# Loading a weight stream in neighbouring pairs of chunks: one 1 MB transfer into two of four slots, in place of two of 512 KB

## The reference, cut to what matters

```python
for l in range(DEPTH):                            # 2 layers
    mc = adaln(c_ctx, ada_w[l], ada_b[l])         # silu(c) @ ada_w: (1024) x (1024, 6144)
    ml = adaln(c, ada_w[l], ada_b[l])             # shift, scale, gate for both halves of the layer
    h = modulate(x, norm_mix[l], m[0], m[1])      # rmsnorm(x) * (1 + scale) + shift
    y = retention_mixer(h, ...) if l == 0 else attention(h, ...)
    x = x + m[2] * y
    h = modulate(x, norm_ffn[l], m[3], m[4])
    a = conv3(h @ ffn_w_in[l]); u, g = split(a)   # D_FF = 2816
    x = x + m[5] * ((silu(g) * u) @ ffn_w_out[l])
y = rmsnorm(x, norm_final)
```

## Time and profile before

| | us |
|---|---|
| median of 3 runs | 2169.85 (2168.47 to 2174.03) |
| the profiled execution | 2169.51 |
| its span | 2167.7 |
| TensorE busy (PE, 12352 matmuls) | 2075.3 (96%) |
| VectorE busy | 957.8 (44%) |
| ScalarE busy | 654.2 (30%) |
| GpSimd busy | 662.3 (31%) |
| mean granted clock of TensorE | 0.977 |

### The profile page before, as it was taken

How to read it: one execution, slowest core, us unless ns; L and a number is a source line. 1 busy time by engine, 2 the same in 40 slices (tenths; PEclk the granted TensorE clock), 3 DMA queues, 4 the chain that set the end, 5 groups by cost and what they waited for, 6 DMA issues and landing times.

```text
span 2167.7 us, 32212 instructions
## 1 busy us (share of the span) xinstructions
PE 2075.3 (96%) x12352; PEld 1816.5 (84%) x12352; DVE 957.8 (44%) x1420; ACT 654.2 (30%) x1282; POOL 662.3 (31%) x400
## 2 busy tenths in 40 slices
PE   5899999999999998999999999899989999999998
PEld 2776887698588757999999999895559999999998
DVE  1502420340241044662564363657651773574473
ACT  2432222212222314331232233334432432232232
POOL 2333233223323313333323324430004433333332
PEclk8899999999999998999999999899999999999999
DMA  6532232222233201442432342220002122222221
GB/s 251 182 123 68 102 113 68 97 91 85 68 108 107 69 31 52 142 144 76 139 136 87 107 145 69 67 82 1 1 1 69 58 78 78 69 77 78 68 68 50
DMA packets 52440, 190.01 MB, mean 88 GB/s; under 512 B 5872, under 2 KB 7152, under 8 KB 51696
## 3 DMA queue, kind: packets, MB, share of 16 engines
q1 hardware_dynamic: 47232, 171.99, 23.7%
q10 hardware_dynamic: 5104, 16.53, 2.0%
HBM read 181.41 MB, written 7.08 MB: 87 GB/s over the span
## 4 chain that ended last, share of the span: by engine, by line
PE 90%; issue 2%; DVE 2%; DMA 1%; ACT 1%; POOL 1%; POOLq 1%; ACTq 0%; DVEq 0%; SPq 0%
PE ps L349 35%; PE ps L388 21%; PE ps L364 16%; PE ps L700 2%; PE ps L404 2%; PE ps L331 2%; PE ps L540 2%; PE ps L549 1%; PE ps L666 1%; PE ps L683 1%; PE ps L535 1%; PE ps L336 1%; PE ps L422 1%; DMA raw<-stream_dram 1%; PE ps L412 1%
## 5 line engine op out<-in xcount | busy, mean ns | idle before, releaser
L1042 POOL TENSOR_TENSOR w_l<-raw,w_h 128x1024 fp32r<-128x1024 f32 x232 | 563.6, 2431 | 1323.4 <-ACT w_h L735 1323.1
L349 PE MATMUL ps<-h_h,w_h 128*128 128x320 f32 x1696 | 527.6, 311 | 3.6 <-issue 2.1
L349 PE MATMUL ps<-h_h,w_l 128*128 128x320 f32 x1696 | 524.1, 309 | 0.0
L349 PE MATMUL ps<-h_l,w_h 128*128 128x320 f32 x1696 | 523.9, 309 | 0.0
L735 ACT CAST w_h<-raw 128x1024 fp32r<-128x1024 f32 x232 | 245.6, 1059 | 580.4 <-PE ps L388 315.2
L349 PEld LDWEIGHTS ps<-h_h,w_h 128*128 128x128 f32 x1696 | 318.4, 188 | 16.8 <-issue 15.2
L349 PEld LDWEIGHTS ps<-h_l,w_h 128*128 128x128 f32 x1696 | 318.5, 188 | 0.2 <-issue 0.2
L349 PEld LDWEIGHTS ps<-h_h,w_l 128*128 128x128 f32 x1696 | 318.4, 188 | 0.0
L1192 DVE SCALAR_TENSOR_TENSOR xT<-ps,mods,xT 128x128 f32<-128x128 f32 (+2 forms) x264 | 108.0, 437 | 302.2 <-PE ps L388 302.2
L1333 DVE SCALAR_TENSOR_TENSOR cc<-ca,vec,cc 128x641 f32<-128x641 f32 x88 | 231.3, 2629 | 15.2 <-issue 15.2
L388 PE MATMUL ps<-m_l,w_h 128*128 128x320 f32 x704 | 217.0, 308 | 0.0
(11 more groups left out here) (186 smaller groups left out, 2706.7 us busy)
## 6 DMA issues: line engine op xcount, KB each, us to landing
raw<-stream_dram SPq DMA_DIRECT2D x328, 512.0 KB, 3.5
S<-state_dram ACTq DMA_DIRECT2D x4, 1024.0 KB, 7.5
new_state_dram<-st_out ACTq DMA_DIRECT2D x8, 512.0 KB, 3.1
xT<-x_dram ACTq DMA_DIRECT2D x1, 2560.0 KB, 11.7
y_dram<-aq ACTq DMA_DIRECT2D x8, 320.0 KB, 2.4
dm<-diff_dram ACTq DMA_DIRECT2D x1, 512.0 KB, 4.0
rope_t<-rope_t_dram ACTq DMA_DIRECT2D x1, 512.0 KB, 7.6
rope_a<-rope_a_dram ACTq DMA_DIRECT2D x1, 512.0 KB, 3.5
```

The source lines that it names most:

```text
L349: mm = nc.tensor.matmul(ps[:, banks + half, 0:HALF], w, x[:, k, lo_hi(half)], start=(k == 0 and n == 0), stop=(k == KT - 1 and n == 2))
L1042: nc.gpsimd.tensor_tensor(w_l[:, r, :], raw[:, s, :], w_h[:, r, :].bitcast(F32), ALU.subtract).then_inc(raw_used[s], 1)
```

## The change

Neighbouring chunks c and c + 1 (c even) are loaded by one DMA of 1 MB into slots c % 4 and c % 4 + 1. SP waits for `raw_used` of both slots first. The two slots of a pair share one landing semaphore, so whoever waits for either chunk waits for the whole megabyte. The stream lies in memory pair by pair, with 8 KB in a row for each partition. There are 164 DMAs in place of 328. Nothing else differs: `raw_landed[s]` is now a name for the pair's semaphore, and the counts that consumers wait for are the same, since each slot is still filled once in every four chunks.

```diff
-        raw_landed = [sem(f"raw_landed{s}") for s in range(RAW)]
+        pair_landed = [sem(f"pair_landed{s}") for s in range(RAW // 2)]
+        raw_landed = [pair_landed[s // 2] for s in range(RAW)]
...
             def load(c, i, turns):
-                s = c % RAW
                 if turns is not None:
-                    sp.wait_ge(raw_used[s], turns)
-                sp.dma_start(raw[:, s, :], dr["stream"][c + RAW * i]).then_inc(raw_landed[s], 16)
-
-            for c in range(RAW):
+                    sp.wait_ge(raw_used[c], turns)
+                    sp.wait_ge(raw_used[c + 1], turns)
+                sp.dma_start(raw[:, c:c + 2, :], dr["stream"][c // 2 + RAW // 2 * i]).then_inc(pair_landed[c // 2], 16)
+
+            for c in range(0, RAW, 2):
                 load(c, 0, None)
             with sp.Fori(1, CHUNKS // RAW) as i:
-                for c in range(RAW):
+                for c in range(0, RAW, 2):
                     load(c, i, i)
...
     stream = np.concatenate(parts)
     assert stream.shape == (CHUNKS, P, CH), stream.shape
+    stream = stream.reshape(CHUNKS // 2, 2, P, CH).transpose(0, 2, 1, 3)
```

## The result

| | before | after |
|---|---|---|
| median, us | 2171.19 (4 runs) | 2195.85 (4 runs, 2195.27 to 2198.67) |
| the profiled execution | 2169.51 | 2195.84 |
| its span | 2167.7 | 2194.1 |

The ratio is 1.0112, with a 95% interval of 1.0100 to 1.0125: 24 us slower, where 23 were forecast. Every page line of the changed kernel stands one line lower in the file (L303 is the load, L405 the block).

What follows compares the result with a forecast made beforehand. TensorE was taken as the bound, with 90% of the chain; loads cost only where they land late. Blocks 21.9 plus start 1.5 gave 23.4 us on 2169.5, so 2192.9, stated as 2193; range 2183 to 2208.

Steps and rivals of the forecast that it cites:

- The forecast's 14 blocks: Blocks behind the start whose last a chunk has its cover used up or nearly so; together 21.9 us longer.
- start, to the block at 102.37: Program start, loads on the chain: chunks 10 and 11 +0.7, first four m chunks +0.8; sum +1.5, between -2 and +5.
- the v blocks of heads 0 to 3: Attention's v blocks: heads 1 to 3 lose 5.0 us together, head 0 loses 1.1.
- E: Extra landing time of a pair's second 512 KB: 1.25 us, so a pair lands 4.65 us after issue.
- `S` as an upper bound: The 1 MB load of `S` took 7.2 us, bounding the extra landing time from above at 3.8.
- The rivals at E = 0 and 3.8: A pair lands as fast as a chunk: 2174, chance 0.06; or it lands like `S`: 2233, chance 0.06.
- the fourth, a megabyte in 4 KB pieces: Rival: the megabyte goes out as 4 KB pieces at full cost, 2193 to 2199; chance 0.05.
- a2's 0.43 us: In late blocks the third a chunk, wanted 0.43 us before the fourth, lands with it and adds that much.
- the first turns of the second and third group: Two feed-forward blocks whose fourth a chunk lands 0.33 us after the start; 1.18 us each, 2.4 together.
- "Cost 0" for the casts behind a block: First m chunk behind a block: ScalarE's cast ends 1.7 us later, but ScalarE's next work moves equally; cost 0.
- The rival of a gain at the start: The start is bandwidth-bound and gains 3.7 us at the higher rate: 2188; chance 0.08.

Runs made afterwards that it cites:

- Giving the cover back: Changed kernel with its feed-forward blocks one m chunk later (ten of the eleven move): 1.0076 to the kernel before, 16 to 17 us slower.
- The shared landing alone: Kernel before, still with single 512 KB loads, but the two chunks of a pair share a semaphore and consumers wait for both: 1.0024, 5 us.
- the constants first: Changed kernel with ScalarE issuing the load of the constants ahead of that of x: 1.0101 to the kernel before, 21 to 22 us.
- joint issue with separate landings: SP waits for both slots of a pair as in the change, then issues two 512 KB loads with a semaphore each: 1.0088 to the kernel before, 19 us.

## Why the prediction was right

**Place and mechanism.** The forecast's 14 blocks are the 14 that became longer, and the six others behind the start still take 1.92 us. Behind the last block only 1.1 us are lost, to the granted clock (below). Giving the cover back brought the feed-forward blocks back to 1.92; the kernel with only the blocks in pairs puts 14 of the 24 us there (10 to 19).

**Where the 26.3 us between the two profiled executions are:**

| | forecast | profile after |
|---|---|---|
| start, to the block at 102.37 | 1.5 | 4.9 |
| the v blocks of heads 0 to 3 | 6.1 | 0.7 + 0.9 + 0.8 + 1.0 = 3.4 |
| the first stalled feed-forward block (887.20) | 1.7 | 3.3 |
| the other nine | 14.1 | 12.2 |
| between the blocks and behind them | 0 | 2.5 |
| sum | 23.4 | 26.3 |

So the sum is right in part by luck: two terms were too large, two too small, and one was missing.

**E was too small.** 1.25 was forecast from two loads of 512 KB, and a landing of 4.65 us; lone 1 MB loads land 4.8 to 5.0 us after their issue, 1.4 more than the 3.3 to 3.5 of before. `S` as an upper bound was far off, as its neighbours suggested. The rivals at E = 0 and 3.8 are out. So is the fourth, a megabyte in 4 KB pieces: the stream's queue moves 171.98 MB in 23616 packets, where it took 47232.

**A term that was wrong: a2's 0.43 us.** I took a2 to be wanted 0.43 before a3, and so to cost that much more when both land together. In every kernel that I compared a block ends 1.1 us after the landing of its last chunk, or 1.92 after its start where that is later (the block of 887.20 apart, where the granted clock had fallen, see below). Before, the block at 918.64 has its a3 1.03 us after its start and ends at 2.12; after, the block at 1085.46 has its pair at 2.49 and ends at 3.61. Two chunks left or one, the rest takes the same 1.1 us: the rows above show eight matmuls in 1.07 behind the landing, and four in 1.05. The shared landing alone leaves the blocks as they were. A late block thus pays E, 1.3 to 1.6 us, not 1.68; the first turns of the second and third group, which had margin, pay 0.9 and 1.0 (the nine together: 12.2). In the v blocks of heads 0 and 1 there was margin too. In heads 2 and 3 there was none, but the single load had already taken 4.1 us there and the megabyte took 4.8 and 5.0, so that E was only 0.7 and 0.9. I had added 1.25 to a landing of 4.1 as to one of 3.4. E was too small and a2's share too large; that the two come near to cancelling in a late block (1.68 forecast, 1.3 to 1.6 measured) is luck.

**"Cost 0" for the casts behind a block failed once.** I looked at a turn in the middle of the loop, where ScalarE is idle before the cast. In the first turn it isn't idle behind it: the evacuation and VectorE's convolution hang on that cast, and the cast that frees a3's slot on them. The block of 887.20 lost 3.3 in place of 1.7. The traces split it: its last load is issued 0.87 us before the block's start in place of 2.33 (1.5 us), takes 4.79 in place of 3.50 (1.3), and the block ends 1.67 behind the landing in place of 1.10 (0.6), because the clock has fallen, next. With m chunks alone in pairs it lost 1.1, with blocks alone 1.2.

**The missing term is TensorE's granted clock.** Windows of the kernel after, around that block (PE busy, PEld, DVE, ACT, POOL, then PEclk, DMA share, GB/s):

```profile
895.00:900.00 5.00, 2.11 (x19) 1.01 (x21) 3.70 (x6) 0.77 (x2) 0.00 (x0) 1.00 0.77 275
900.00:904.00 4.00, 4.00 (x19) 2.60 (x16) 2.79 (x4) 3.04 (x6) 0.00 (x0) 0.57 0.72 246
904.00:908.00 4.00, 4.00 (x30) 4.00 (x29) 0.42 (x1) 0.00 (x0) 2.66 (x1) 1.00 0.49 199
```

TensorE stood for 2.9 us there, and then the clock granted to it fell from 2.4 to 1.2 GHz for 3.4 us: beside the 0.6 us in the block itself, the next block starts another 1.0 us later than the stall alone explains. With the constants first it happened again: 3.0 us of idle TensorE in this block, then 3.4 at the low level. The stalls of up to 1.6 us in the other turns left the clock at 1.00. In the record of the granted clock two further stretches at the low level, one behind the retention and one around the attention's end, are 3.4 us longer than before and cost 1.0 and 1.1. That these are the change's is not shown: the first is absent in two of the kernels with single loads and as long as here where only the start is in pairs, and the second varies as much.

**The start.** Windows of the start, first of before, then of after, then of the shared landing alone:

```profile
17.00:80.00 63.00, 45.51 (x248) 32.59 (x240) 21.06 (x44) 26.71 (x62) 20.53 (x11) 0.78 0.57 198
```

```profile
17.00:80.00 63.00, 44.61 (x223) 32.39 (x216) 19.64 (x41) 24.50 (x52) 21.82 (x12) 0.65 0.53 188
```

```profile
17.00:80.00 63.00, 44.32 (x228) 32.63 (x224) 20.40 (x41) 24.86 (x55) 20.64 (x11) 0.65 0.52 188
```

The kernel after and the one with the shared landing alone have a mean granted clock of 0.65 there and lose 4.9 and 4.1 us; before has 0.78. The transposing step (L412, eight matmuls) shows the level by its length, timelines of before and of after:

```profile
27.21 1.05 PE L412 MATMUL ps<-cst,ada_o 128*128 128x2 f32 x8 [0.79 <-DVE ada_o L1169]
33.56 1.07 PE L412 MATMUL ps<-cst,ada_o 128*128 128x2 f32 x8 [0.80 <-DVE ada_o L1169]
```

```profile
28.85 1.86 PE L413 MATMUL ps<-cst,ada_o 128*128 128x2 f32 x8 [0.84 <-DVE ada_o L1170]
35.93 1.87 PE L413 MATMUL ps<-cst,ada_o 128*128 128x2 f32 x8 [0.84 <-DVE ada_o L1170]
```

Two such steps and block 4 (3.44 us for 2.22) make 2.8 of the 4.9 us; the constants land 0.7 us later; the 1.4 left I put down to landings and casts, about what I had forecast, without having tested it. Two kernels point to the shared wait: single transfers with a shared landing lose 4.1, joint issue with separate landings nothing. But neither the cause nor the size is settled: the kernels with single loads at the start reach block 4 between 2.5 us earlier and 0.7 us later than before, and the block of 102.37 between 2.3 earlier and 1.9 later. With only the start in pairs 2.1 us are lost; with the constants first the pairs' loss is gone, though there the three transposing steps ahead of block 4 are all 1.87 us long, so at the low level. I can't say from these runs what decides it.

**Bandwidth.** The rival of a gain at the start, the Trainium skill's rule to batch to 1 MiB (DMA: Bandwidth & Descriptors, "Measured (HBM→SBUF, 128 partitions, SWDGE, issued from GpSimd)"), is out: from 17 to 80 us the queues move 188 GB/s in place of 198. The landing of 4.9 us, of loads issued by SP, lies under the 6.15 us listed there for a megabyte issued by GpSimd. The rule is about bytes per second; where the blocks stall the queues have time to spare (from 895 to 1310 us the DMA engines are 32% busy), and the last two chunks of a block had not.

## What to carry to other kernels

Before merging two loads, find the consumer with the least cover and ask when each half can be issued: the merged load goes out when the later slot is free, and the later half lands behind the earlier one's bytes. Where the cover of a load is one piece of work and used up, the 1.4 us more are paid in full, each time; where it is several, the merging costs nothing and here brought nothing either. Moving the consumer back gave the cover again and took it from the casts behind it, so 8 of 24 us came back; more slots in `raw` were not tried. A shared landing cost nothing in the late blocks, and something where an engine stood behind the pair: in the first cast of the loop and, it seems, at the start. A long stall can cost again through the granted clock.

## What the runs showed of the hardware that I had not expected

- 512 KB alone: 3.3 to 3.5 us from issue to landing; 1 MB alone in 8 KB rows: 4.8 to 5.0. Two loads of 512 KB issued together: in the feed-forward turns the second lands 4.6 to 4.9 after the first issue, so the transfer's size itself made next to no difference.
- Matmuls of 32 columns by 512 behind a landing: four took 1.05 us, eight 1.07, at the high level of the clock: four more added 0.02.
- Stalls of TensorE of 2.9 and 3.0 us in the same block of two kernels were followed by 3.4 us at 1.2 GHz, those of up to 1.6 us in the other turns were not.
